# Decoder trunk on one core: cache copies taken out of the samples' steps, late window rows awaited later, and the samples' softmax divided behind the values

## The chip, the core and the metric

The kernel runs on one core of a Trainium2 chip. The metric is the device time of one execution in microseconds (us); lower is better. Matrix products run on TensorE (PE; its weight loads are PEld), elementwise work and reductions on VectorE (DVE), activations and scaled copies on ScalarE (ACT), cross-partition work on GpSimd (POOL). SyncE (SP) computes nothing here and issues nearly all DMA transfers, in the order of its program.

## The reference, cut to what matters

One layer of a decoder trunk, in float32, for 256 prompt rows and for 8 samples of 4 new rows each (width 1024). The part that the change touches is the windowed attention of the samples:

```python
def _dilated_branch_sample(q, k_all, v_all, window, dil, rel_bias):
    ...
    logits = jnp.einsum('bthd,btjhd->bhtj', q, kg, preferred_element_type=jnp.float32) + bias[None, :, None, :]
    logits = jnp.where(valid[None, None], logits, NEG)
    lse = jax.nn.logsumexp(logits, axis=-1)
    p = jnp.exp(logits - lse[..., None])
    o = jnp.einsum('bhtj,btjhd->bthd', p.astype(v_all.dtype), vg)
    return o, lse.transpose(0, 2, 1)
...
        xs = xs + _mix_out(o_a, o_b, w_out[l])
        xs = xs + _cross_attn(_rmsnorm(xs, g_x[l]), cache_mem_k[l], cache_mem_v[l], w_xq[l], w_xo[l])
        xs = xs + _moe(_rmsnorm(xs, g_ff[l]), *moe_w)
        n_new = k.shape[1]
        kw_s.append(k_all[:, n_new:])
        vw_s.append(v_all[:, n_new:])
```

There are three branches (window and dilation 128/1, 512/4, 2048/16), 8 heads of 64. The outputs `k_win_sample` and `v_win_sample` are each sample's old window of 2048 rows moved on by its 4 new rows, so nearly all of both caches is written out again. After the attentions a router sends each of the 288 rows to 4 of 32 experts, whose weights (12 MB each, float32) are read from DRAM in full.

## The kernel before, in words

Every engine has its own program, written out in order by hand, with semaphores between them; no scheduler reorders it. The stages are: norm and input projection; seven sample steps `for b in range(1, DEC_B)`; the output projection `w_out` (`out`); cross-attention (`xq` first); router; experts 0 to 31.

**A sample step b** holds, side by side, the scores of sample b and the values of sample b-1, one unit of the prompt's attention (`scores`, `logits`, `share`, `turned`, `unit_values`), and "fills" (`FILL`): pieces of the prompt's memory keys (`mk`) and values (`mv`), 16 matmuls each, which have nothing to do with the samples. For sample b, PE multiplies out the query for each of 4 tokens t (`row(b, t)` on PE, job `qb`), DVE multiplies it with the window's keys in two products and reduces the result (`row` on DVE: L1169, L1170, then the reduction L1176). `logits(b)` on DVE belongs to the prompt unit. POOL finds the maximum, ACT takes exponentials (`sample_exp`). DVE then adds them up per partition (`sums`, L1145), POOL adds over partitions, and DVE divides (`shares`, L1149 and L1150); these quotients `pr` are PE's stationary operand in `values` (L1684, 12 matmuls, and L1682, 4). DVE masks the result (`keep`, L1161) and PE turns it (`turn_values`, L1692, job `pvt`).

**Windows.** A sample's keys (K) and values (V) come as 128x2048 plus three 32x2048 transfers (L512, L515) into one buffer each. SP issues V(b) when the values matmuls of b-1 are through, and K(b+1) when the scores of b are. ACT then forms the last 128 rows of each ("late" rows, L787) by copying them; DVE waits for `late_k` ahead of the first product of a sample, PE for `late_v` ahead of the first value matmul.

**Banks.** PSUM products go round a ring of 7 banks (`TURN = 7`). The list `jobs`, filled by `add`, gives job number n the bank n % 7. `take(pe, ...)` makes PE wait until the job 7 places earlier has been read out of that bank. Bank 7 (`sx_bank`) lies outside of the ring.

**Copies.** The moved-on caches are written by 32 copies from DRAM to DRAM of 2044 KB each (`copy`, L494), issued by SP between its other transfers. `COPIES` says how many go at each of 14 places; what is left goes in `copy(len(pieces))` right behind `step0()`, which issues the first expert's weights; the loop over the other experts (L628) follows. The loads of the identity matrix and of the input rows stand at the head of SP's program.

Of the kernel before, what the change touches and what calls it, by code (L numbers as in the profile page):

```python
# [8 lines left out]
P = 128  # L9
# [43 lines left out]
def constants():  # L53
# [22 lines left out]
    col = np.arange(AW)  # L76
    own = ((p[:, None] // 32 == p[:, None] // 8 % 4) & (p[:, None] % 8 == col[None, :] // HD)).astype(np.float32)
    diag = np.concatenate([own, (p[:, None] // 32 == np.arange(DEC_T)[None, :]).astype(np.float32)], 1)
# [20 lines left out]
def build(nc, i, o):  # L99
# [5 lines left out]
    with ctx:  # L105
# [86 lines left out]
        zs = small[:, 320:352]  # L192
        zz = small[:, 352:384]
        stat = small[:, 384:440]

        own = hn[:, 2, 0:AW + DEC_T]
# [79 lines left out]
        COPIES = [5, 1, 3, 1, 2, 2, 2, 2, 2, 2, 3, 2, 1, 3]  # L276
# [30 lines left out]

        add("pt", DEC_B - 1)
        add("pvt", DEC_B - 2), add("o", DEC_B - 1), add("out", 0, 0), add("out", 0, 1), add("pv", DEC_B - 1)
# [99 lines left out]
        zpart = sem("zpart")  # L409
        zall = sem("zall")  # L410
        prob = sem("prob")
# [56 lines left out]

        block = ctx.enter_context(nc.Block())
# [3 lines left out]
        def _(sp):  # L473
            load(sp, "ident", ident[:, :], i["c_ident"])
            for t in (0, 2, 1):
# [177 lines left out]
        def _(pool):  # L653
# [23 lines left out]
            for b in range(DEC_B):  # L677
# [8 lines left out]
                pool.wait_ge(zpart, b + 1)  # L686
                nc.gpsimd.partition_all_reduce(zz, zs, P, bass.bass_isa.ReduceOp.add).then_inc(zall, 1)
# [60 lines left out]
        def _(act):  # L748
# [12 lines left out]

            act.wait_ge(consts, 2)
# [97 lines left out]

            def sample_out(b):
# [14 lines left out]
            for b in range(1, DEC_B):  # L876
                unit_pt(b - 1)
                if b >= 2:
                    sample_out(b - 2)
# [4 lines left out]
                unit_out(b - 1)  # L884
                unit_exp(b)
# [4 lines left out]
            unit_pt(DEC_B - 1)  # L890
            sample_out(DEC_B - 2)
            unit_out(DEC_B - 1)
            late_values(DEC_B - 1)
            sample_exp(DEC_B - 1)
# [3 lines left out]
            for t, (t0, n) in enumerate(TOK):  # L898
                if t == 1:
                    sample_out(DEC_B - 1)  # L900
# [109 lines left out]
        def _(dve):  # L1010
# [132 lines left out]
            def sums(b):  # L1143
                dve.wait_ge(sexp, b + 1)
# [893 lines left out]
```

## Time and profile before

| | us |
|---|---|
| time, median of 3 runs | 1411.29 |
| the 3 runs | 1403.95 to 1412.52 |
| profiled execution: its own time | 1409.75 |
| profiled execution: span | 1408.0 |
| PE busy | 1255.7 (89%) |
| DVE busy | 481.2 (34%) |
| ACT busy | 230.3 (16%) |
| chain that ended last: DMA, PE, DVE | 55%, 35%, 5% |

The profile is one execution; its span runs from the first to the last instruction and its own time is 1.75 us longer. Busy shares are over the whole span, of which the experts take the last two thirds. Positions below are in us from the start of the span: the sample steps lie at about 97 to 254, `out` and cross-attention follow, the second expert's weights are asked for at 467. "L1684" is a line of the kernel before.

### The profile page before, as it was taken

How to read it: one execution, taken by the hardware profiler on the slowest of the kernel's cores; microseconds unless marked ns; L12 is line 12 of the kernel's file. 1: busy time of each engine (PE TensorE's matmuls, PEld its weight loads, DVE VectorE, ACT ScalarE, POOL GpSimd, SP SyncE). 2: the span in 40 equal slices, each digit the busy share in tenths (PEclk: the TensorE clock that was granted, in tenths of full speed). 3: DMA queues.
4: the chain of work that ended last, by engine and by line, in shares of the span. 5: the costliest groups of instructions: out<-in, count | busy, mean ns of one | idle time of the engine just before them, and what ended most of it. 6: DMA issues, size and time to landing. Idle time of an engine off the chain costs nothing.

```text
span 1408.0 us, 16530 instructions
## 1 busy us (share of the span) xinstructions
PE 1255.7 (89%) x6407; PEld 528.5 (38%) x6407; DVE 481.2 (34%) x1037; ACT 230.3 (16%) x448; POOL 67.7 (5%) x69
## 2 busy tenths in 40 slices
PE   7989877989897999998999989999899998999986
PEld 5444323456644433333333333333333333333332
DVE  2387888332326412312232122321223212132124
ACT  1334443211311110110110100110011010011102
POOL 2010000005007000000000000000000000000000
PEclk9999988999997999999999999999999999999998
DMA  9999999998989699999999999999999999999993
GB/s 339 353 381 363 399 397 379 361 370 306 360 354 344 254 431 427 427 429 426 429 428 429 429 429 429 428 430 427 430 427 430 427 429 428 429 429 429 429 428 158
DMA packets 51740, 557.14 MB, mean 396 GB/s; under 512 B 7021, under 2 KB 9301, under 8 KB 15885
## 3 DMA queue, kind: packets, MB, share of 16 engines
q1 hardware_dynamic: 50629, 553.04, 96.0%
q0 software_dynamic: 1072, 3.57, 0.6%
q8 instruction: 26, 0.43, 0.1%
q14 instruction: 13, 0.11, 0.0%
HBM read 552.02 MB, written 71.72 MB: 443 GB/s over the span
## 4 chain that ended last, share of the span: by engine, by line
DMA 55%; PE 35%; DVE 5%; ACT 2%; issue 1%; SPq 1%; DVEq 0%; ACTq 0%; PEldq 0%
DMA wide<-in_w_gate_up 49%; PE bank L1954 12%; DMA wide<-in_cache_v_win 3%; PE bank L1642 3%; PE bank L1983 2%; PE bank L1684 2%; PE bank L1749 2%; PE bank L1512 2%; PE bank L1508 1%; PE bank L1662 1%; DMA slim<-in_w_xq 1%; DMA slim<-in_w_xv 1%; ACT wide L787 1%; PE bank L1737 1%; PE bank L1791 1%
## 5 line engine op out<-in xcount | busy, mean ns | idle before, releaser
L1954 PE MATMUL bank<-wide,att 128*64 128x512 f32 x2048 | 463.3, 596 | 58.5 <-DMA wide<-in_w_gate_up 58.3
L1954 PEld LDWEIGHTS bank<-wide,att 128*64 128x64 f32 x2048 | 139.3, 136 | 362.5 <-issue 228.8
L1983 PE MATMUL bank<-slim,att 128*64 128x512 f32 x1024 | 226.8, 595 | 0.0
L1422 DVE TENSOR_SCALAR att<-bank 128x512 f32<-128x512 f32 x32 | 22.1, 691 | 469.0 <-PE bank L1954 469.0
L1983 PEld LDWEIGHTS bank<-slim,att 128*64 128x64 f32 x1024 | 70.6, 137 | 152.2 <-issue 149.2
L1401 DVE TENSOR_TENSOR x<-x,bank 128x512 f32<-128x512 f32 x68 | 46.6, 685 | 233.1 <-PE bank L1936 226.4
L980 ACT ACTIVATE att<-att 128x512 f32<-128x512 f32 x32 | 20.2, 630 | 517.6 <-DVE att L1422 517.6
L1936 PE MATMUL bank<-tb,att 128*128 128x512 f32 (+1 forms) x192 | 84.7, 611 | 1.8 <-ACT tb L989 1.3
L989 ACT ACTIVATE tb<-bank 64x512 f32<-64x512 f32 x64 | 37.8, 591 | 234.1 <-PE bank L1983 233.7
L1662 PE MATMUL bank<-slim,ta 128*128 128x512 f32 x128 | 57.8, 601 | 0.5 <-DMA slim<-in_w_xv 0.3
L1176 DVE TENSOR_REDUCE small<-wide 128x24 f32<-128x1536 f32 x28 | 49.1, 1753 | 1.0
L1684 PE MATMUL bank<-wide,pr 128*32 128x512 f32 x192 | 33.0, 840 | 17.5 <-ACT wide L787 11.4
L1903 PE MATMUL bank<-att,mkT 128*128 128x128 bf16 x408 | 46.3, 223 | 1.4 <-DVE att L1352 1.4
L1903 PE MATMUL bank<-att,ta 128*128 128x128 bf16 x408 | 45.7, 222 | 0.0
L787 ACT ACTIVATE wide<-wide 32x512 f32<-32x512 f32 x60 | 37.6, 626 | 44.3 <-DMA wide<-in_cache_v_win 24.5
L1169 DVE TENSOR_TENSOR wide<-wide,bank 128x1024 f32<-128x1024 f32 x28 | 33.9, 1210 | 6.0 <-PE bank L1568 3.9
L1662 PEld LDWEIGHTS bank<-slim,ta 128*128 128x128 f32 x128 | 23.4, 190 | 33.4 <-issue 29.7
L1903 PEld LDWEIGHTS bank<-att,mkT 128*128 128x128 bf16 x408 | 28.3, 99 | 15.2 <-issue 14.6
L1749 PE MATMUL bank<-ta,slim 128*128 128x288 f32 x128 | 31.6, 408 | 2.7 <-DMA slim<-in_w_xq 1.8
L1429 DVE TENSOR_TENSOR att<-att 128x512 f32<-128x512 f32 x32 | 33.4, 1044 | 1.1
L985 ACT ACTIVATE att<-bank 128x512 f32<-128x512 f32 x32 | 19.1, 597 | 74.9 <-PE bank L1974 74.9
L1974 PE MATMUL bank<-ident,att 128*128 128x128 f32 x128 | 21.0, 286 | 11.5 <-DVE att L1429 9.6
(290 smaller groups left out, 1153.1 us busy)
## 6 DMA issues: line engine op xcount, KB each, us to landing
wide<-in_w_gate_up SPq DMA_DIRECT2D x128, 2048.0 KB, 25.4
slim<-in_w_down SPq DMA_DIRECT2D x64, 2048.0 KB, 22.0
out_k_win_sample<-in_cache_k_win SPq DMA_DIRECT2D x16, 2044.0 KB, 25.3
out_v_win_sample<-in_cache_v_win SPq DMA_DIRECT2D x16, 2044.0 KB, 22.9
wide<-in_w_in SPq DMA_DIRECT2D x8, 1024.0 KB, 15.8
wide<-in_cache_v_win SPq DMA_DIRECT2D x8, 1024.0 KB, 7.5
wide<-in_cache_mem_k SPq DMA_DIRECT2D x8, 1024.0 KB, 24.4
wide<-in_cache_mem_v SPq DMA_DIRECT2D x8, 1024.0 KB, 14.7
```

Source lines behind the costliest of these rows:

```text
L787: ins = A(late[32 * s:32 * s + 32, :], win[96:128, s, :], ACT.Copy)
L989: ins = A(ye[i // 2][CAP * (i % 2):CAP * (i % 2) + CAP, 512 * h:512 * h + 512], bank_y[CAP * h:CAP * h + CAP, :], ACT.Copy)
L1176: link(V.tensor_reduce(S_[b % 2][:, :, t, :], pd.rearrange("p k (h d) -> p k h d", d=HD), AX.X, ALU.add))
L1401: ins = V.tensor_tensor(dst, dst, bk[:, :], ALU.add)
L1642: ins = M(tk[h][0][0:n, :], left[:, k, t0:t0 + n], slim[:, k, 512 * h:512 * h + 512], start=k == 0, stop=k == KC - 1)
L1662: ins = M(ps[:, :], ta[:, k, P * t:P * t + P], slim[:, k, 512 * h:512 * h + 512], start=k == 0, stop=k == KC - 1)
L1684: ins = M(ps[g, :], flat[:, kind, :], vwin[:, 8 if kind == 2 else 4 * kind + t, :], start=k == 0, stop=False)
L1749: ins = M(ps[:, 0:T], slim[:, k, P * c:P * c + P], ta[:, k, :], start=k == 0, stop=k == KC - 1)
L1903: M(bk[:, c:c + 2 * CAP], hparts[t][:, s, P * k:P * k + P], onehot[:, t, :], start=t == 0 and s == 0, stop=False)
L1936: ins = M(out, back[buf][:, t0:t0 + m], ye[buf][:, 512 * h:512 * h + 512], start=True, stop=True)
L1954: ins = M(bk[half[h], :], rows[:, k, :], wide[:, k, c:c + 512], start=False, stop=k == KC - 1)
L1983: ins = M(bank_y[half[h], :], aT[:, f % 4, f // 4, :], slim[:, f, 512 * h:512 * h + 512], start=f == 0, stop=f == KC - 1)
```

## The change

- `COPIES`: one copy more before the first step (6 instead of 5 at its first place), one fewer at the third place, one fewer in each of the steps 2, 4, 5 and 6; one more at each of two places in cross-attention and the router, and three instead of one left for the place behind `step0`.
- The identity matrix and one block of input rows are loaded from ACT's queue instead of SP's; the mask `c_diag` shrinks from 128x516 to 128x32.
- DVE awaits `late_k` only ahead of the product that uses the late rows; PE takes the late rows third and awaits `late_v` there.
- `sums`, the addition on POOL, `shares` and `keep` on DVE go. PE forms the sums with 16 one-column matmuls ahead of the values (the same stationary `pr`, streaming a column of ones, into column b of bank 7), DVE takes one reciprocal of 128x1 (`part_of_sum`), and `keep` becomes a scaled copy on ACT. `turn_values` is 8 matmuls with 64 columns of weights instead of 4 with 128. Values start when the exponentials are there.
- `pvt` moves behind `unit_values`, on PE and in `jobs`, and the end of the last step is put in another order. One small product (`toep`) moves ahead of ten others. The prompt's shares stay on DVE.

The core of the diff:

```diff
-        COPIES = [5, 1, 3, 1, 2, 2, 2, 2, 2, 2, 3, 2, 1, 3]
+        COPIES = [6, 1, 2, 1, 1, 1, 1, 1, 2, 2, 4, 2, 2, 3]
...
             add("qb", b, 2), add("pt", b - 1)
+            for f in FILL[b, 0]:
+                add(*f)
+            add("qb", b, 3), add("o", b - 1)
             if b >= 2:
                 add("pvt", b - 2)
-            for f in FILL[b, 0]:
-                add(*f)
-            add("qb", b, 3), add("o", b - 1), add("s", b, 0), add("s", b, 1)
+            add("s", b, 0), add("s", b, 1)
...
+            def keep(b):
+                if b:
+                    b_, use = place(("pvt", b - 1))
+                    act.wait_ge(bank_full[b_], use + 1)
+                act.wait_ge(rz_in, b + 1)
+                ps, s = product(act, "pv", b)
+                A(kept, ps[:, :], ACT.Copy, scale=rz[:, b:b + 1]).then_inc(s, 1)
...
+            def part_of_sum(b):
+
+                b_, use = place(("pv", b))
+                dve.wait_ge(bank_full[b_], use + 1)
+                V.reciprocal(rz[:, b:b + 1], sx_bank[:, b:b + 1]).then_inc(rz_in, 1)
...
+                    if t == 0:
+                        dve.wait_ge(late_k, b + 1)
                     V.tensor_tensor(pd[:, 2, :], kw[:, 8, :], ps[:, :], ALU.mult).then_inc(s, 1)
...
             def values(b):
-                pe.wait_ge(prob, b + 1)
+                pe.wait_ge(sexp, b + 1)
+                pe.wait_ge(rz_in, b)
                 pe.wait_ge(v_in, 64 * (b + 1))
-                pe.wait_ge(late_v, b + 1)
                 ps, s = take(pe, "pv", b)
...
-                for k, kind in enumerate((2, 0, 1, 3)):
+                for kind in range(4):
+                    for t in range(DEC_T):
+                        n = NS if kind == 3 else P
+                        M(sx_bank[32 * t:32 * t + 32, b:b + 1], flat[0:n, kind, :], ones[0:n, 0:1], start=kind == 0, stop=kind == 3,
+                          tile_position=(0, 32 * t))
+                for k, kind in enumerate((0, 1, 2, 3)):
+                    if kind == 2:
+                        pe.wait_ge(late_v, b + 1)
...
             turned(DEC_B - 1)
-            turn_values(DEC_B - 2)
             unit_values(DEC_B - 1)
             round_[0] = 3
             read_out(pe, "o", DEC_B - 1)
             rows_times("out", 0, tb, P, 0)
+            turn_values(DEC_B - 2)
             values(DEC_B - 1)
```

How the order of instructions changes is shown at three places. First PE in step 3, from the fills to the values of sample 2, with the bank numbers of the ring and the waits. L1568 (L1563 after) is a query's product for one token, L1668 (L1663) a fill, L1692 (L1696) `turn_values`, L1684 (L1686) the values, L1676 the one-column matmuls; L1615 and L1591 belong to the prompt unit. Before:

```order
L1668 MATMUL bank2<-ident,hn 128x128 [waits bank_free2,bank_free6]
L1668 MATMUL bank2<-ident,hn 128x128 x3
L1568 MATMUL bank3<-hn 128x512 [waits bank_free3]
L1615 MATMUL bank4<-scr,att 64x128 [waits bank_free4,bank_free6]
L1615 MATMUL bank4<-scr,att 64x128
L1591 MATMUL bank5<-att 128x256 [waits bank_free5]
L1591 MATMUL bank6<-att 128x256 [waits bank_free6]
L1568 MATMUL bank0<-hn 128x512 [waits bank_free0]
L1568 MATMUL bank1<-hn 128x512 [waits bank_free1]
L1684 MATMUL bank2<-wide,pr 32x512 [waits late_v,bank_free2,v_in,prob]
```

After:

```order
L1563 MATMUL bank2<-hn 128x512 [waits bank_free2]
L1610 MATMUL bank3<-scr,att 64x128 [waits bank_free3,bank_free6]
L1610 MATMUL bank3<-scr,att 64x128
L1696 MATMUL bank4<-hn,wide 64x4 [waits bank_free4,bank_free3]
L1696 MATMUL bank4<-hn,wide 64x4 x7
L1586 MATMUL bank5<-att 128x256 [waits bank_free5]
L1586 MATMUL bank6<-att 128x256 [waits bank_free6]
L1563 MATMUL bank0<-hn 128x512 [waits bank_free0]
L1563 MATMUL bank1<-hn 128x512 [waits bank_free1]
L1676 MATMUL bank7<-ones,pr 32x1 [waits v_in,bank_free2,rz_in,sexp]
```

The values' bank 2 was last used by a fill before, and is last used by the query of the fourth token, `qb(3, 3)`, after the change.

Second, DVE in step 3, over the same time: L1169 and L1170 (L1164 and L1167 after) are a token's two products, L1176 (L1175) its reduction, L1121 and L1125 (L1130 and L1134) the prompt unit's `logits`. Before:

```order
L1161 TENSOR_TENSOR wide<-bank,hn 128x512 [waits dve_done,bank_full5]
L1169 TENSOR_TENSOR wide<-wide,bank 128x1024 [waits bank_full4]
L1170 TENSOR_TENSOR wide<-wide,bank 128x512
L1176 TENSOR_REDUCE small<-wide 128x3x8 [waits bank_free4]
L1145 TENSOR_REDUCE small<-pr 128x32 [waits sexp,dve_done]
L1169 TENSOR_TENSOR wide<-wide,bank 128x1024 [waits bank_full0]
L1170 TENSOR_TENSOR wide<-wide,bank 128x512
L1176 TENSOR_REDUCE small<-wide 128x3x8 [waits bank_free0]
L1149 RECIPROCAL small<-small 128x32 [waits zall,dve_done]
L1150 TENSOR_TENSOR pr<-pr,small 128x128 [waits dve_done]
L1121 TENSOR_TENSOR scr<-bank,att 128x128 [waits bank_full5,bank_full4]
```

After:

```order
L1156 RECIPROCAL small<-bank 128x1 [waits dve_done,bank_full5]
L1164 TENSOR_TENSOR wide<-wide,bank 128x1024 [waits bank_full4]
L1167 TENSOR_TENSOR wide<-wide,bank 128x512
L1175 TENSOR_REDUCE small<-wide 128x3x8 [waits bank_free4]
L1164 TENSOR_TENSOR wide<-wide,bank 128x1024 [waits bank_full0,dve_done]
L1167 TENSOR_TENSOR wide<-wide,bank 128x512
L1175 TENSOR_REDUCE small<-wide 128x3x8 [waits bank_free0]
L1130 TENSOR_TENSOR scr<-bank,att 128x128 [waits bank_full5,bank_full4,dve_done]
L1130 TENSOR_TENSOR scr<-bank,att 128x128 [waits bank_full6]
L1134 TENSOR_REDUCE small<-scr 128x1 [waits bank_free5]
L1134 TENSOR_REDUCE small<-scr 128x1 [waits bank_free6]
L1164 TENSOR_TENSOR wide<-wide,bank 128x1024 [waits bank_full2]
```

Four of DVE's instructions have gone from the step, and a short reciprocal has come; the last row after the change is the fourth token's first product, from bank 2.

Third, SP ahead of the first step: L494 (L491 after) are the copies, L512 (L509) is the window of keys of the next sample. Before:

```order
L494 DMA out_k_win_sample<-in_cache_k_win 16x8x4088 x2
L494 DMA out_v_win_sample<-in_cache_v_win 16x8x4088 x2
L494 DMA out_k_win_sample<-in_cache_k_win 16x8x4088
L373 DMA att<-toep_dram 128x8x256 [waits squares,toep_out]
L498 DMA slim<-in_w_xk 128x1024 x6
L494 DMA out_k_win_sample<-in_cache_k_win 16x8x4088
L512 DMA wide<-in_cache_k_win 128x2048 [waits w_read]
```

After:

```order
L491 DMA out_k_win_sample<-in_cache_k_win 16x8x4088 x2
L491 DMA out_v_win_sample<-in_cache_v_win 16x8x4088 x2
L491 DMA out_k_win_sample<-in_cache_k_win 16x8x4088 x2
L372 DMA att<-toep_dram 128x8x256 [waits squares,toep_out]
L495 DMA slim<-in_w_xk 128x1024 x6
L491 DMA out_v_win_sample<-in_cache_v_win 16x8x4088
L509 DMA wide<-in_cache_k_win 128x2048 [waits w_read]
```

Ahead of the window K(1) there stand seven copies instead of six.

## Rows read from the trace of the kernel before

**Rows 1.** Busy by stretch: PE, PEld, DVE, ACT, POOL; then clock, DMA share, GB/s.

```profile
97.00:250.00 153.00, 124.70 (x584) 54.69 (x584) 129.96 (x194) 64.28 (x148) 10.04 (x19) 0.89 1.00 383
205.00:210.00 5.00, 5.00 (x29) 1.12 (x22) 4.83 (x9) 2.50 (x4) 0.43 (x1) 0.68 1.02 384
250.00:455.00 205.00, 180.23 (x975) 112.73 (x971) 71.86 (x152) 41.68 (x87) 48.30 (x32) 0.91 0.93 352
455.00:467.00 12.00, 10.12 (x85) 6.62 (x84) 7.06 (x44) 0.95 (x6) 0.00 (x0) 0.76 0.04 16
560.00:1300.00 740.00, 679.46 (x3555) 243.67 (x3553) 177.10 (x390) 75.79 (x122) 0.00 (x0) 1.00 1.01 428
```

**Rows 2.** SP's issues of copies: start, duration, engine, line, tile.

```profile
32.73 1.34 SPq L494 DMA_DIRECT2D out_k_win_sample<-in_cache_k_win  x2
...
35.40 0.60 SPq L494 DMA_DIRECT2D out_k_win_sample<-in_cache_k_win  x1
```

**Rows 3.** DMA issues at 32.7:33.2 and 35.3:36.1: KB each, us to landing.

```profile
out_k_win_sample<-in_cache_k_win SPq DMA_DIRECT2D x1, 2044.0 KB, 14.9
...
out_k_win_sample<-in_cache_k_win SPq DMA_DIRECT2D x1, 2044.0 KB, 37.4
```

**Rows 4.** Chain of waits at the first sample step.

```profile
84.83 8.81 DMA wide<-in_cache_k_win
...
97.51 1.22 DVE wide L1169
```

**Rows 5.** SP's issues of V windows 1, 3 and 7.

```profile
120.42 0.33 SPq L512 DMA_DIRECT2D wide<-in_cache_v_win  x1
...
166.22 0.33 SPq L512 DMA_DIRECT2D wide<-in_cache_v_win  x1
...
251.24 0.33 SPq L512 DMA_DIRECT2D wide<-in_cache_v_win  x1
```

**Rows 6.** Chain of waits, step b=5.

```profile
190.52 10.34 DMA wide<-in_cache_v_win
```

**Rows 7.** PE in step b=5; idle before each, with releaser, in brackets.

```profile
188.72 7.13 PE L1662 MATMUL bank<-slim,ta 128*128 128x512 f32 x16
...
196.36 0.95 PE L1692 MATMUL bank<-hn,wide 128*128 128x4 f32 x8
...
199.99 0.61 PE L1568 MATMUL bank<-hn 96*128 96x512 bf16 x2 [1.44 <-DVE wide L1170]
203.68 4.99 PE L1684 MATMUL bank<-wide,pr 128*32 128x512 f32 x24 [3.09 <-ACT wide L787]
208.61 1.06 PE L1682 MATMUL bank<-att,pr 32*32 32x512 f32 x8
```

**Rows 8.** DVE in step b=5.

```profile
192.19 0.69 DVE L1161 TENSOR_TENSOR wide<-bank,hn 128x512 f32<-128x512 f32 x1 [0.21 <-DVE pp L1139]
...
197.83 0.37 DVE L1145 TENSOR_REDUCE small<-pr 128x32 f32<-128x128 f32 x1 [1.44 <-ACT pr L859]
...
199.96 1.75 DVE L1176 TENSOR_REDUCE small<-wide 128x24 f32<-128x1536 f32 x1
201.75 0.35 DVE L1149 RECIPROCAL small<-small 128x32 f32<-128x32 f32 x1
...
203.66 1.21 DVE L1169 TENSOR_TENSOR wide<-wide,bank 128x1024 f32<-128x1024 f32 x1
204.79 0.68 DVE L1170 TENSOR_TENSOR wide<-wide,bank 128x512 f32<-128x512 f32 x1
```

**Rows 9.** PE, values of sample 0.

```profile
116.59 2.78 PE L1684 MATMUL bank<-wide,pr 128*32 128x512 f32 x24
```

**Rows 10.** PE, values of sample 6 and start of cross-attention.

```profile
245.74 4.45 PE L1684 MATMUL bank<-wide,pr 128*32 128x512 f32 x24 [5.64 <-ACT wide L787]
...
305.80 4.39 PE L1749 MATMUL bank<-ta,slim 128*128 128x288 f32 x17 [1.81 <-DMA slim<-in_w_xq]
```

**Rows 11.** SP's issue of the second expert's weights.

```profile
467.00 6.96 SPq L628 DMA_DIRECT2D wide<-in_w_gate_up  x2
```

More of the change, by code:

```diff
@@ L473, in _ @@
         def _(sp):
-            load(sp, "ident", ident[:, :], i["c_ident"])
-            for t in (0, 2, 1):
+            for t in (0, 2):
                 t0, n = TOK[t]
@@ L878, in _ @@
                 if b >= 2:
-                    sample_out(b - 2)
+                    keep(b - 2)
                 sample_exp(b - 1)
@@ L890, in _ @@
             unit_pt(DEC_B - 1)
+            unit_out(DEC_B - 1)
+            keep(DEC_B - 2)
+            sample_exp(DEC_B - 1)
+            late_values(DEC_B - 1)
             sample_out(DEC_B - 2)
-            unit_out(DEC_B - 1)
-            late_values(DEC_B - 1)
-            sample_exp(DEC_B - 1)
             act.wait_ge(stored["mk"], 16)
@@ L899, in _ @@
                 if t == 1:
+                    keep(DEC_B - 1)
                     sample_out(DEC_B - 1)
@@ L1191, in _ @@
             dve.wait_ge(k_in[0], 64)
-            dve.wait_ge(late_k, 1)
             for t in range(DEC_T):
@@ L1200, in _ @@
             dve.wait_ge(k_in[1], 64)
-            dve.wait_ge(late_k, 2)
             row(1, 0), shift(0)
@@ L1214, in _ @@
                         share(0, 1, P)
-                    if t < 3:
-                        (shift, sums, shares)[t](b - 1)
-                    if b >= 2 and t == 0:
-                        keep(b - 2)
+                    if t == 0 and b > 1:
+                        shift(b - 1)
+                        part_of_sum(b - 2)
                     if t == 2:
@@ L1223, in _ @@
             share(DEC_B - 1, DEC_B, P * (UNITS[DEC_B - 1][1] + 1))
-            shift(DEC_B - 1), keep(DEC_B - 2), sums(DEC_B - 1), shares(DEC_B - 1)
+            shift(DEC_B - 1), part_of_sum(DEC_B - 2)
             for u in range(2):
@@ L1252, in _ @@
                 if t == 0:
-                    keep(DEC_B - 1)
+                    part_of_sum(DEC_B - 1)
                 norm(5 + t, n, x[0:n, t, :], hn[0:n, t, :], 6 + t)
@@ L1491, in _ @@
             pe.wait_ge(rb_rep, 1)
+            ps, s = take(pe, "toep")
+            M(ps[0:HEADS, 0:TOEP], rb, cb[:, 0:TOEP], start=True, stop=True).then_inc(s, 1)
             for kind in range(6):
@@ L1497, in _ @@
                 M(sx_bank[0:NS, 304 + 8 * t:312 + 8 * t], cb[:, c:c + NS], rb, start=True, stop=True)
-            ps, s = take(pe, "toep")
-            M(ps[0:HEADS, 0:TOEP], rb, cb[:, 0:TOEP], start=True, stop=True).then_inc(s, 1)
             for t in range(3):
@@ L1690, in turn_values @@
                 ps, s = take(pe, "pvt", b)
-                for c in range(4):
-                    ins = M(ps[:, 4 * c:4 * c + 4], kept[:, P * c:P * c + P], own[:, AW:AW + DEC_T], start=True, stop=True)
+                if b == 0:
+                    pe.wait_ge(loaded["diag"], 16)
+                for h in range(HEADS):
+                    ins = M(ps[64 * (h % 2):64 * (h % 2) + 64, 4 * (h // 2):4 * (h // 2) + 4], kept[:, HD * h:HD * h + HD],
+                            own[:, DEC_T * h:DEC_T * h + DEC_T], start=True, stop=True)
                 ins.then_inc(s, 1)
@@ L1706, in _ @@
                 turned(b - 1)
-                if b >= 2:
-                    turn_values(b - 2)
                 for f in FILL[b, 0]:
@@ L1712, in _ @@
                 unit_values(b - 1)
+                if b >= 2:
+                    turn_values(b - 2)
                 scores(b)
```

42 lines of the change are left out of this document (13 added, 29 removed).

## The prediction

> **What bounds the kernel now.** I read the busy times by stretch first, to see which resource has no slack where, then the chain of waits for what a step ends on, then PE, DVE and SP in one sample step. Over the experts the DMA share is 1.01 at 428 GB/s, and PE is busy 679 of 740 us. That stretch has no slack in the queue, and the change doesn't touch it: the end moves by as much as the second expert's weights start earlier or later, at 467.00 [rows 11]. Just before that, from 455 to 467, the DMA share is 0.04: the queue is empty, and it is PE and DVE that are late. So time saved in the steps reaches the end one for one, as long as the queue isn't made late itself. During the steps (97 to 250) the queue has a share of 1.00, DVE is busy 130 of 153 us and PE 125 [rows 1]: three resources near their limits, and which of them closes a step is the question.
>
> Before, it is the V window. V lands 10.34 us after its last issue, behind two copies [rows 6], ACT copies its late rows, PE has waited 3.09 us for them, and the values (4.99 + 1.06 us) end where the next V is issued [rows 7]. Six such intervals last from 120.42 to 251.24: 45.8 us for the first two, 85.0 for the last four, which hold the mv fills [rows 5].
>
> **Copies.** A copy costs the queue 6.3 us: the first of five lands at 32.73 + 14.9 = 47.6, the last, issued just behind 35.40, at 35.4 + 37.4 = 72.8, and 25.2 / 4 = 6.3 [rows 2, 3]. One fewer in steps 4 to 6 brings V forward by about that, more than the 3.09 us that PE waits: the V wait goes, and it is no longer what is late.
>
> The copy that is added at the first place stands ahead of K(1). K(1) is on the chain: it lands at 84.83 + 8.81 = 93.64, the late rows follow on ACT, and DVE's first product starts at 97.51 [rows 4]. So this copy delays the first step by up to 6.3 us. To its credit stand a smaller mask (my estimate from the copy's price and size: 0.4 us) and two loads fewer at the head of SP's program (0 to 1 us). I take **+5.0**, bounds +4.3 to +6.3. That DVE awaits `late_k` only at the third product doesn't help: a product of ACT that PE waits for stands behind the late rows in ACT's order, so the first product is as late as ever.
>
> The Trainium skill, "DMA: Bandwidth & Descriptors", section "Issuing engines are not separate DMA queues", says that a load started from another engine runs on the same DMA engines and saves only the time of issuing it. By that rule the two loads on ACT are worth nothing in the queue, and the credit would be 0.4; the trace of before has no such load to test it.
>
> Four copies net go from the steps to behind 250. The queue has 7% of 205 us idle there, 14 us, and 11.5 of the 12 us ahead of 467 [rows 1]: 26 us for 4 x 6.3 = 25. It fits just, though not exactly where the idle lies. The two copies behind `step0` fill the gap ahead of 467; of the two earlier ones some part is absorbed, and the queue comes free at about 473 instead of 467. SP's first two issues there take 6.96 us before [rows 11], since the second one awaits a buffer, so most of these 6 us lie beside that wait. I take **+0.7**, bounds 0 to +6.
>
> **DVE.** A step loses keep 0.69, sums 0.37 with a wait of 1.44 for ACT's exponentials, a reciprocal 0.35, and a multiplication about as long [rows 8]. A reciprocal of 128x1 comes; about 3.0 us go in all. Of the 20.8 us from V to V, DVE's own list then fills 17.7. POOL's addition and its wait vanish with it; ACT takes on the scaled copy, some 0.7 us, with 3 us to spare before V's landing.
>
> **PE's new wait.** The bank numbers show one that the diff doesn't name. `pv(b-1)` now takes the bank of `qb(b,3)`, so the values of b-1 can't begin before DVE has finished the third product of the fourth token (the row that begins at 203.66 before [rows 8]); before, the bank had last held a fill that had long been read. Behind the values stand, on PE, the fill and then the next step's third-token query, which DVE needs. This makes a closed loop between PE and DVE: values 2.78 + 1.06 at full clock [rows 9] or 4.99 + 1.06 at low clock [rows 7]; the one-column matmuls, u; a fill, 7.13 less its overlap with what follows, or 7.0 [rows 7]; a query 0.4; then on DVE the third token, 1.21 + 0.68 + 1.75, or 3.6, logits about 1.05 (1.3 between the divisions and 203.66, less for the prompt units with one tile), and the fourth token's products, 1.8 [rows 8]. Without u: 17.6 at full clock, 19.8 at low.
>
> u has no row. 16 matmuls make 32 records. Four column groups can run side by side, as the values' do (24 records of 512 columns in 2.78 us). Then there are 8 rounds: `turn_values` has 8 records with four columns in 0.95 us [rows 7], with four times the weight columns, so 0.45 to 0.95. One after the other at that row's pace it would be 3.8 us. I take **0.7**, since the column groups are what the values use too, with the same stationary tile. So a step is 18.3 at full clock and 20.5 at low.
>
> "TensorEngine Tiling (Array Packing)" in the Trainium skill, section "Instruction Overhead", states that a matmul with one streamed column takes as long as one with 60. By that, 8 rounds stay within the 0.7, and 32 in a line give the rival below; no row here has a one-column product.
>
> **The sum**, at low clock in the values, as before shows it (granted clock 0.68 in 205 to 210 [rows 1]). First two intervals: about +0.1 (the one-column matmuls against DVE's relief). Of the last four (85.0): the first, which held other waits as well, -1.5; the next two from 20.8 to 20.5, -0.6 together; the last -4.5, since the values of sample 6 take another bank and wait no longer for V, where 5.64 us stand before [rows 10]. With +5.0 of the first copy that is -1.5 when V(7) is issued. After that, `turn_values` (0.95) and the one-column matmuls (0.7) stand among the `out` products, +1.65, and the 1.81 us wait for w_xq [rows 10] goes, as w_xq no longer trails so many copies; with +0.7 from the late copies, about -1.
>
> The clock decides over the rest. At full clock in the values five steps gain 2.2 us each, 11 more, to about -12 at most. Before, PE idles 1.44 and 3.09 us ahead of the values [rows 7] and the clock is low; after, it waits about 4 us in the same place, for DVE. So low remains likelier; I count some 30% of the steps at full, -3. **Forecast: -4 on the profiled 1409.75, or 1406.** Its own range is 1401 to 1411. The profiled execution stands 1.5 below the median of 1411.29; a run of before at 1403.95 shows how far one execution strays, and differences under about 1% (14 us) can hardly be told from no change.
>
> **Rivals.**
>
> *The clock stays up, or the bank wait costs nothing.* If the values run at full clock all through, steps are 18.3; if besides the one-column products hide, they follow DVE's list at 17.7. Five steps of 2.2 to 2.8 us on top of -1: 1395 to 1399. For it: PE has less to wait for in all. Against it: the wait is gathered in one place.
>
> *The one-column matmuls run one after the other (slower).* 32 records in a line at that row's 119 ns make u 3.8, and at half of it, for a stationary tile a quarter as wide (an estimate), 1.9. From u = 1.0 at low clock a step exceeds 20.8, and every step loses. At 1.9 it is +1.2 at each of seven places, +8 on the sum; at 3.8 +3.1, or +22. That gives 1417 to 1430, slower than before. For it: all use the same 128 rows of the array. Against it: the values' four groups do run side by side.
>
> *The copies are given back late.* If the queue comes free at 473 and nothing hides it, +6 instead of +0.7: 1411. For it: 26 us of idle for 25 of copies is no margin. Against it: the second expert's weights aren't needed at once, since PE has the whole of expert 0 before it.
>
> **Chances.** Forecast 0.48, clock or DVE's list 0.22, copies given back 0.15, one after the other 0.15. Faster by over 1% (below 1397) takes the better half of the first rival and a little of the forecast for an unknown I haven't priced: 0.18. Slower by over 1% (above 1425) needs the upper third of this slow rival: 0.05. The range, 1396 to 1418, leaves out the lower end of the one and the upper half of the other.
>
> **What would show it.** V waits ahead of the values gone, in their place an idle time of PE ended by DVE's L1167; V(1) about 5 us later than 120.42, and V(7) near 250; steps of 20.5 us where the clock is low in the values and 18.3 where it isn't; the one-column matmuls side by side in under 1 us; the queue busy up to 470 and more, with no gap from 455. Wrong would be: steps that end in a V wait still (a copy priced too low), a K(1) that DVE doesn't wait for, and a stream of weights that starts much later than 473.

## The result and the profile after

The changed kernel takes 1414.46 us in the median of 17 runs (1412.69 to 1417.75), the kernel before 1406.59 in 17 (1402.61 to 1412.52): a ratio of 1.0054, interval 1.0041 to 1.0067. The time lies in the range that was given, but the forecast was 0.3% faster than the kernel before, and it came out 0.54% slower. The profiled execution of the changed kernel takes 1412.69 with a span of 1410.9, 2.9 us more than before. Single executions of these two kernels lie up to 5.9 us off their own medians (of the kernel before, two profiled ones took 1409.75 and 1409.74, some 3 us above its median), so the traces are good for tracing where the mechanism went, and the ratios for how much.

Busy times by stretch in the changed kernel, to set beside [rows 1]; the last three columns are granted clock, DMA share and GB/s:

```profile
97.00:110.00 13.00, 6.79 (x26) 4.85 (x26) 5.92 (x11) 7.92 (x16) 2.86 (x4) 0.50 1.02 426
97.00:250.00 153.00, 129.38 (x864) 59.73 (x864) 117.58 (x167) 71.36 (x159) 6.03 (x11) 0.86 0.79 314
250.00:455.00 205.00, 179.07 (x1010) 110.32 (x1006) 73.67 (x155) 42.97 (x89) 47.78 (x31) 0.91 1.01 375
455.00:467.00 12.00, 10.02 (x82) 7.75 (x84) 5.61 (x36) 0.95 (x6) 0.34 (x1) 0.66 1.01 372
```

The queue that was full from 97 to 250 now idles a fifth of that time, and what idled later is full: 1.01 from 250 to 467, with no gap left ahead of the second expert. The first row is the surprise: TensorE ran at 0.50 for the whole first stretch of the steps, its lower level of 1.2 GHz.

The chain of waits at the first step shows why, beside [rows 4]. The window of keys lands at 80.75 + 18.09 = 98.84, 5.2 us later than before:

```profile
80.75 18.09 DMA wide<-in_cache_k_win
```

PE at the same place; the number in brackets is how long it had idled, and what ended it:

```profile
80.47 10.46 PE L1569 MATMUL bank<-wide,ta 128*128 128x512 f32 x24
102.16 1.19 PE L1563 MATMUL bank<-hn 96*128 96x512 bf16 x2 [11.23 <-ACT att L769]
```

PE is through with its front at 90.9 and stands still for 11.23 us, for a product of ACT that comes behind the late rows of the window. Behind that the clock is low: 0.51 over 94 to 110 and 0.76 from there to 120, where the kernel before has 1.00 in both in the execution shown. A second execution of it has 0.68 over 94 to 110 (last run below).

SP's issues of the windows V(1), V(3), V(6) and V(7), as in [rows 5]:

```profile
129.28 0.33 SPq L509 DMA_DIRECT2D wide<-in_cache_v_win  x1
...
174.91 0.33 SPq L509 DMA_DIRECT2D wide<-in_cache_v_win  x1
...
236.14 0.33 SPq L509 DMA_DIRECT2D wide<-in_cache_v_win  x1
...
250.36 0.33 SPq L509 DMA_DIRECT2D wide<-in_cache_v_win  x1
```

V(1) is 8.9 us later than before, the next two intervals take 45.6 (45.8 before), the last four 75.5 (85.0), and V(7) is 0.9 earlier. One step in the middle, PE, beside [rows 7]:

```profile
205.49 0.60 PE L1563 MATMUL bank<-hn 96*128 96x512 bf16 x2
209.82 0.71 PE L1676 MATMUL bank<-ones,pr 128*32 128x1 f32 x32 [3.72 <-DVE wide L1167]
210.45 4.46 PE L1686 MATMUL bank<-wide,pr 128*32 128x512 f32 x24
```

and DVE over the same time, beside [rows 8]:

```profile
202.90 1.22 DVE L1164 TENSOR_TENSOR wide<-wide,bank 128x1024 f32<-128x1024 f32 x1 [2.52 <-PE bank L1563]
...
207.86 1.21 DVE L1164 TENSOR_TENSOR wide<-wide,bank 128x1024 f32<-128x1024 f32 x1
208.99 0.68 DVE L1167 TENSOR_TENSOR wide<-wide,bank 128x512 f32<-128x512 f32 x1
```

No wait for V is left. PE waits 3.72 us for DVE's L1167 ahead of the one-column products, that is for the third product of the fourth token, whose bank it wants. DVE in turn waited 2.52 us for the query at 202.90 that stands behind the fill on PE. The 32 records of the one-column products take 0.71 us.

The end of the steps. DVE's last score rows and the prompt's last share:

```profile
243.47 1.22 DVE L1164 TENSOR_TENSOR wide<-wide,bank 128x1024 f32<-128x1024 f32 x1 [3.04 <-PE bank L1563]
...
252.94 0.74 DVE L1140 TENSOR_TENSOR scr<-scr,small 128x512 f32<-128x512 f32 x1
```

and PE around it, with the output projection (L1637; before it starts at 254.10) and the first product of cross-attention (L1754, beside [rows 10]):

```profile
249.24 1.06 PE L1684 MATMUL bank<-att,pr 32*32 32x512 f32 x8
253.73 1.16 PE L1600 MATMUL bank<-hn,scr 128*128 128x128 f32 x8 [3.44 <-DVE scr L1140]
...
257.09 16.26 PE L1637 MATMUL bank<-slim,tb 128*128 128x512 f32 x32 [0.39 <-ACT tb L837]
...
308.80 1.78 PE L1754 MATMUL bank<-ta,slim 128*128 128x288 f32 x3 [0.69 <-DVE ta L1055]
```

The values of sample 6 are through at 250.3, and PE then stands 3.44 us for the prompt's last share. `out` starts 3.0 us later than before, runs with the clock low in its first part (granted 0.53 over 257 to 262; 16.26 us for 32 products, 14.00 before at 1.00), and cross-attention starts 3.0 us later than in [rows 10]. The second expert's weights are asked for at 468.85 (467.00 in [rows 11]), and they land 10.6 us after their issue, where it was 7.2 before. The columns are size and us from issue to landing:

```profile
wide<-in_w_gate_up SPq DMA_DIRECT2D x1, 2048.0 KB, 10.6
```

### The profile page after: what moved, and what is told of

The parts are those of the page before. It is cut to its first block, busy times and chain, and to the rows that moved or that the text cites. A ratio compares the mean times of both kernels' runs of the same rounds, so it can differ in the third digit from the quotient of the medians.

```text
span 1410.9 us, 17140 instructions
## 1 busy us (share of the span) xinstructions
PE 1257.9 (89%) x6727; PEld 530.2 (38%) x6727; DVE 470.8 (33%) x1013; ACT 235.4 (17%) x456; POOL 63.5 (5%) x61
## 4 chain that ended last, share of the span: by engine, by line
DMA 51%; PE 35%; DVE 7%; SPq 5%; issue 1%; ACT 1%; DVEq 0%
DMA wide<-in_w_gate_up 49%; PE bank L1959 12%; PE bank L1657 4%; PE bank L1637 3%; PE bank L1988 2%; SPq L495 2%; PE bank L1754 2%; PE bank L1686 2%; SPq L372 1%; DMA wide<-in_cache_k_win 1%; DVE wide L1164 1%; DMA hn<-in_mem_prompt 1%; PE bank L1742 1%; PE bank L1941 1%; DVE small L1175 1%
## 5 line engine op out<-in xcount | busy, mean ns | idle before, releaser
L989 ACT ACTIVATE att<-att 128x512 f32<-128x512 f32 x32 | 20.2, 630 | 518.5 <-DVE att L1417 518.5
L1175 DVE TENSOR_REDUCE small<-wide 128x24 f32<-128x1536 f32 x28 | 49.1, 1753 | 1.0
L1164 DVE TENSOR_TENSOR wide<-wide,bank 128x1024 f32<-128x1024 f32 x28 | 33.9, 1211 | 31.7 <-PE bank L1563 31.6
L1754 PE MATMUL bank<-ta,slim 128*128 128x288 f32 x128 | 33.3, 425 | 0.7 <-DVE ta L1055 0.7
L1686 PE MATMUL bank<-wide,pr 128*32 128x512 f32 x192 | 30.7, 789 | 0.0
## 6 DMA issues: line engine op xcount, KB each, us to landing
out_v_win_sample<-in_cache_v_win SPq DMA_DIRECT2D x16, 2044.0 KB, 27.6
```

Source lines behind the costliest of these rows:

```text
L1164: V.tensor_tensor(pd[:, 0:2, :], pair, ps[:, :].unsqueeze(1).broadcast_to([P, 2, AW]), ALU.mult)
L1175: link(V.tensor_reduce(S_[b % 2][:, :, t, :], pd.rearrange("p k (h d) -> p k h d", d=HD), AX.X, ALU.add))
L1686: ins = M(ps[g, :], flat[:, kind, :], vwin[:, 8 if kind == 2 else 4 * kind + t, :], start=k == 0, stop=False)
L1754: ins = M(ps[:, 0:T], slim[:, k, P * c:P * c + P], ta[:, k, :], start=k == 0, stop=k == KC - 1)
```

## The experiments

Twelve runs followed. Ratios are to the kernel before on the same chip, with a 95% interval; the changed kernel stands at 1.0054. The expectations name times beside 1406.6 for the kernel before; in the second set of four runs its median was 1408.6, in the third 1407.1, so go by the ratios.

### The copies, apart and together

Four kernels differ from the changed one or from the one before in the list alone:

```diff
 changed        [6, 1, 2, 1, 1, 1, 1, 1, 2, 2, 4, 2, 2, 3]
 before         [5, 1, 3, 1, 2, 2, 2, 2, 2, 2, 3, 2, 1, 3]
+first_back     [5, 1, 3, 1, 1, 1, 1, 1, 2, 2, 4, 2, 2, 3]  in the changed kernel
+late_back      [6, 1, 2, 1, 2, 2, 2, 2, 2, 2, 3, 2, 1, 3]  in the changed kernel
+copies_back    [5, 1, 3, 1, 2, 2, 2, 2, 2, 2, 3, 2, 1, 3]  in the changed kernel
+copies_only    [6, 1, 2, 1, 1, 1, 1, 1, 2, 2, 4, 2, 2, 3]  in the kernel before
```

`first_back`, what was expected:

> The changed kernel with one number moved back: the copy that was added ahead of K(1) goes where it was, behind the first windows (places one and three of COPIES are 5 and 3 again); the four copies that were moved behind the steps stay there. Reference points: before 1406.6, changed 1414.5. Three theories. START (the loss is the first step, which begins 5 us later and at the lower clock, V(1) issued at 129.3 instead of 120.4): 1406, V(1) near 120. LATE QUEUE (the loss is the copies given back behind 250, where the queue of the changed kernel has no gap left, share 1.01 in every stretch): 1412 to 1415, the earlier first step is lost again at the queue. REWRITING (the loss lies in the bank wait and the one-column products, the copies are even): 1414.

1.0023 (1.0007 to 1.0038), 1409.7 us. By the medians more than half of the loss is this one copy: 0.31 of 0.54%. START had expected all of it. V(1) and V(7):

```profile
122.62 0.33 SPq L509 DMA_DIRECT2D wide<-in_cache_v_win  x1
...
243.99 0.33 SPq L509 DMA_DIRECT2D wide<-in_cache_v_win  x1
```

Both are 6.4 to 6.7 us earlier than in the changed kernel. V(1) is still 2.2 us later than in the execution shown of the kernel before (0.4 earlier than in its second one), though the window of keys now lands earlier, at 91.9 instead of 93.6: PE idles 4.0 us ahead of it instead of 11.2, and the clock is 0.57 over 94 to 110. The same waits of PE, summed over the span (total, times, longest):

```profile
PE bank L1676 <- DVE wide L1167: 12.2, 5, 3.7
...
PE bank L1563 <- ACT att L769: 4.0, 1, 4.0
```

`late_back`, what was expected:

> The changed kernel with the other half of the copies put back: steps 2, 4, 5 and 6 get their second copy again, and the places behind the steps lose one each (one copy is left behind the first expert's weights); the extra copy ahead of K(1) stays. START: 1414, since the first step is as late as in the changed kernel. LATE QUEUE: 1406 to 1408, with an empty queue ahead of 467 again and steps that are no longer than 20.8. REWRITING: 1414.

1.0049 (1.0028 to 1.0069), 1413.0 us: beside the changed kernel a gain that can't be told from none. LATE QUEUE as the main cause falls.

`copies_back`, what was expected:

> The changed kernel with the list of copies of the kernel before; everything else is as changed. START: 1406. LATE QUEUE: 1406 or somewhat less. If both hold and add up: 1400. REWRITING: 1414. Steps wait for V again (V lands some 10 us after its issue), at 20.5 to 21 us each.

1.0010 (0.9993 to 1.0026), 1408.7 us. With the old list, all the rest of the change together can't be told from no change. V is hardly waited for, 0.7 us in one step, where the expectation had steps that wait for V again. The bank wait is there as in the changed kernel:

```profile
PE bank L1676 <- DVE wide L1167: 12.4, 5, 3.7
```

`copies_only`, what was expected:

> The kernel before with the list of copies of the changed kernel; nothing else is changed. START and LATE QUEUE: 1412 to 1416, as slow as the changed kernel or slower, V(1) near 126. REWRITING: 1406, or less, since the V wait goes and DVE's list of 19 us a step takes its place.

1.0039 (1.0021 to 1.0056), 1411.7 us. REWRITING as the only cause falls too: the list alone makes the old code slower, by an amount that can't be told from the changed kernel's. The V wait has gone, but the steps are 20.0 to 20.8 us as ever, from V(3) to V(7), since PE now waits for DVE's sums and shares. PE in one step:

```profile
204.09 0.60 PE L1568 MATMUL bank<-hn 96*128 96x512 bf16 x2 [1.45 <-DVE wide L1170]
206.59 5.27 PE L1684 MATMUL bank<-wide,pr 128*32 128x512 f32 x24 [1.89 <-DVE pr L1150]
```

V(1) is later than expected, at 130.14 and not near 126. The two loads are still SP's here and PE's front is as late as before, yet PE idles 8.16 us for the late window, and the clock is 0.66 over 94 to 110 and 0.70 to 120. PE's first query product behind the window, and V(1):

```profile
103.65 1.19 PE L1568 MATMUL bank<-hn 96*128 96x512 bf16 x2 [8.16 <-ACT att L772]
```

```profile
130.14 0.33 SPq L512 DMA_DIRECT2D wide<-in_cache_v_win  x1
```

### The bank, the other side of the loop, the front

`ring`: the values take an older bank.

```diff
             add("s", b, 0), add("s", b, 1)
             if b + 1 < DEC_B:
-                add("qb", b + 1, 0), add("qb", b + 1, 1)
+                add("qb", b + 1, 0)
             add("pv", b - 1)
+            if b + 1 < DEC_B:
+                add("qb", b + 1, 1)
...
-                    row(b + 1, 0), row(b + 1, 1)
+                    row(b + 1, 0)
                 values(b - 1)
+                if b + 1 < DEC_B:
+                    row(b + 1, 1)
```

> The changed kernel with the bank wait taken out: the values of sample b-1 come ahead of the second token's query of sample b+1, in the program of PE and in the list of jobs, so that they take a bank that was read out long before, and the query takes the bank of the fourth token. Reference: changed 1414.5. LOOP (the closed loop of PE and DVE sets the steps, and what they lose the end loses): PE no longer waits 1.3 to 3.7 us for DVE's L1167 ahead of the one-column products, steps go from 20.3 to 18 or 19, 1405 to 1408. START (the loss is made ahead of the first step and what the steps gain is lost again at their end): V(1) as late as in the changed kernel at 129, out(0) at most 2 us earlier than 257, 1412 to 1415.

0.9963 (0.9944 to 0.9981), 1403.1 us: 0.9% below the changed kernel and faster than the kernel before. V(3), V(4), V(5) and V(7):

```profile
169.71 0.33 SPq L511 DMA_DIRECT2D wide<-in_cache_v_win  x1
...
186.46 0.33 SPq L511 DMA_DIRECT2D wide<-in_cache_v_win  x1
...
203.62 0.33 SPq L511 DMA_DIRECT2D wide<-in_cache_v_win  x1
...
237.40 0.33 SPq L511 DMA_DIRECT2D wide<-in_cache_v_win  x1
```

Steps of 16.8, 17.1, 19.4 and 14.4 us (V(6) at 222.97), and V(7) 13 us earlier than in the changed kernel. The one-column products follow the query at once, and no wait for L1169, the third product here, stands ahead of them in any step:

```profile
197.43 0.39 PE L1565 MATMUL bank<-hn 96*128 96x512 bf16 x1 [0.77 <-DVE wide L1169]
197.75 0.61 PE L1678 MATMUL bank<-ones,pr 128*32 128x1 f32 x32
```

LOOP holds, with more gain than it had expected (1405 to 1408), and START with its first step as the only loss falls: V(1) is as late as in the changed kernel (129.84), and `out` starts at 245.21, 11.9 us earlier than there. The edit also moves the values ahead of one query on PE, since a job's place in the list gives its bank.

`row2`: the third token's query goes ahead of the fill, on PE and in the list of jobs, and the bank stays shared. The part on PE (the same move in `jobs` is left out):

```diff
             for b in range(1, DEC_B):
-                row(b, 2)
+                if b == 1:
+                    row(b, 2)
                 turned(b - 1)
...
                 values(b - 1)
+                if b + 1 < DEC_B:
+                    row(b + 1, 2)
                 for f in FILL[b, 1]:
                     fill(f)
```

> The changed kernel with the loop cut at its other side: PE multiplies the third token's query of the next sample ahead of the 7 us fill instead of behind it, so that DVE doesn't wait for the fill; the values still take the bank of the fourth token. Reference: changed 1414.5. LOOP: DVE's own list of 17.7 us sets the steps, and its tail before out(0) comes earlier with it: 1400 to 1406. START: 1412 to 1415.

1.0058 (1.0037 to 1.0078), 1417.9 us: no gain. DVE doesn't wait for that query any longer, but the loop closes through the prompt's scores, which stand behind the fill as well. DVE's `logits` with its wait:

```profile
209.10 0.76 DVE L1134 TENSOR_TENSOR scr<-bank,att 128x256 f32<-128x256 f32 x2 [2.28 <-PE bank L1590]
```

and PE's scores (L1590) and the next one-column products:

```profile
208.27 0.70 PE L1590 MATMUL bank<-att 64*128 64x256 f32 x4
...
212.38 0.71 PE L1680 MATMUL bank<-ones,pr 128*32 128x1 f32 x32 [2.87 <-DVE wide L1171]
```

So LOOP's figures failed here, and the trace shows why: this cut was in the wrong place of a loop that stays closed, from the end of the scores over `logits`, the fourth token's products, the values and the fill back to the scores.

`early_window`: the list [4, 1, 4, 1, 2, 2, 2, 2, 2, 2, 3, 2, 1, 3] in the changed kernel.

> The changed kernel with the copies of the kernel before, but 4 instead of 5 of them ahead of the first window of keys (and 4 instead of 3 behind it). In the changed kernel PE is through with its front at 91 and idles 11 us for that window, at the lower clock afterwards. Reference: 1408.7 with 5, 1414.5 as changed. START: the window lands 6 us earlier than with 5, the first rows start at 92 instead of 96, the clock stays up in the first step: 1401 to 1404. Rival (the queue has to carry the copy in any case, right behind the window): 1408.

1.0026 (1.0007 to 1.0046), 1413.0 us, so START's expectation failed and the rival's was not far off. The first step does begin earlier (the first query at 91.4, no longer waiting for the window), with a clock of 0.79 over 94 to 110, but the four copies right behind it stand ahead of V(1), which lands 21.54 us after its last issue; V(2) is issued later than before. SP's issues of V(1) and V(2), and the chain between them:

```profile
117.83 0.33 SPq L509 DMA_DIRECT2D wide<-in_cache_v_win  x1
...
150.76 0.33 SPq L509 DMA_DIRECT2D wide<-in_cache_v_win  x1
```

```profile
119.50 21.54 DMA wide<-in_cache_v_win
```

`loads_back`: the two loads return to SP.

```diff
-            for t in (0, 2):
+            load(sp, "ident", ident[:, :], ident_rows)
+            for t in (0, 2, 1):
...
-            load(act, "ident", ident[:, :], ident_rows)
-            load(act, "x1", x[:, 1, :], second_rows)
```

> The changed kernel with the identity matrix and the second block of input rows loaded by SP again. The changed kernel's PE runs some 5.5 us ahead of the kernel before from the first input product (12.4 instead of 17.7) up to 91, where it waits for the window of keys. START: PE comes 2 to 5 us later to the same wait, which costs nothing, and the lower clock behind it is shorter: 1411 to 1415. Rival (the front counts): slower by those 2 to 5 us, 1417 to 1420.

1.0074 (1.0049 to 1.0098), 1419.8 us; the intervals overlap with the changed kernel's. PE's first input product starts at 17.17 as in the kernel before (17.72), in the changed kernel at 12.38:

```profile
17.17 4.21 PE L1502 MATMUL bank<-ta,wide 128*128 128x288 f32 x8
```

```profile
12.38 3.87 PE L1503 MATMUL bank<-ta,wide 128*128 128x288 f32 x8
```

So the front is faster by nearly 5 us through two loads. How much of that shows in the time these intervals don't tell. START had a shorter stretch of lower clock when PE comes later to the same wait, and that bought nothing. PE idles 6.72 us instead of 11.23, the window lands at 100.16 instead of 98.84, the clock is 0.79 over 94 to 110 and 0.66 to 120, and V(1) comes no earlier, at 131.11 instead of 129.28. PE's first query product behind the window, and V(1):

```profile
103.49 1.19 PE L1562 MATMUL bank<-hn 96*128 96x512 bf16 x2 [6.72 <-ACT att L768]
```

```profile
131.11 0.33 SPq L510 DMA_DIRECT2D wide<-in_cache_v_win  x1
```

### The three together

`ring_first`: `ring` and `first_back` together.

> The changed kernel with two edits: the bank wait taken out (as in the run that had this alone, 0.9963 of the kernel before), and the added copy moved back behind the first windows (alone: 1.0023, where the changed kernel stands at 1.0054). If the first step and the bank wait are two separate losses, they add up: 0.993, some 1397 to 1399 beside 1407 for the kernel before. LATE QUEUE (the queue, full from V(7) on, eats what comes earlier): 0.996, as with the bank wait alone.

0.9944 (0.9930 to 0.9958), 1399.1 us: 0.6% below the kernel before and 1.1% below the changed one. Its two edits gained 0.31% and 0.91% apart; together it is 1.10%. V(1) and V(7):

```profile
122.87 0.33 SPq L511 DMA_DIRECT2D wide<-in_cache_v_win  x1
...
233.07 0.33 SPq L511 DMA_DIRECT2D wide<-in_cache_v_win  x1
```

and the landing of the second expert's first weights, 14 us behind their issue at 449.16 (10.6 in the changed kernel), with the queue full there (DMA share 1.00 from 455 to 467):

```profile
wide<-in_w_gate_up SPq DMA_DIRECT2D x1, 2048.0 KB, 14.0
```

`ring_copies_back`: `ring` with the list of the kernel before.

> The changed kernel with the bank wait taken out and the list of copies of the kernel before, two in each step. THREE LIMITS (the V window behind two copies, DVE's list with the softmax in it and the bank wait each close a step at about 20.5; only with all three gone does it fall to 17): steps of 19.5 to 20.5, waits for V ahead of the values, 1406 to 1409. LOOP alone: 1397 to 1400, since the copies don't matter to the steps.

0.9974 (0.9960 to 0.9989), 1404.4 us. As THREE LIMITS had it, V is waited for again, 2.74, 4.69 and 5.15 us in three steps. The steps are 17.9 to 22.7 us, though, where it had 19.5 to 20.5, and the time lies between its forecast and LOOP's:

```profile
198.10 0.71 PE L1678 MATMUL bank<-ones,pr 128*32 128x1 f32 x32 [2.74 <-DMA wide<-in_cache_v_win]
...
219.54 0.71 PE L1678 MATMUL bank<-ones,pr 128*32 128x1 f32 x32 [4.69 <-DMA wide<-in_cache_v_win]
...
241.89 0.71 PE L1678 MATMUL bank<-ones,pr 128*32 128x1 f32 x32 [5.15 <-DMA wide<-in_cache_v_win]
```

Fewer copies in the steps are worth their place in the kernel whose other two limits are gone: there going from the old list to that of `ring_first` gives 0.3%. With the bank wait still in, the same two lists are `copies_back` (1.0010) and `first_back` (1.0023), and no gain shows. In the old code this list was not run; the changed one, with the copy ahead of K(1), cost 0.4% there.

`ring_fill` has the list [5, 1, 3, 1, 2, 1, 1, 2, 2, 2, 4, 2, 1, 3] in `ring`.

> The bank wait taken out, the added copy moved back, and two of the late copies given to two steps in which the queue still idles half of the time (places five and eight of the list). LATE QUEUE: the queue behind the steps has 12 us less to carry: 1393 to 1396, below the same kernel without this. Rival (V waits behind the second copy in these two steps): as that kernel, 1397 to 1400.

0.9949 (0.9935 to 0.9963), 1400.9 us, as `ring_first`. The rival's figure holds: PE waits 3.7 us for V in one step, and V(7) is issued at 239.53 where `ring_first` has 233.07, so the steps lose 6.5 us.

`before_again`: the kernel before once more.

> The kernel before, unchanged, for a second profile: the one shown is of an execution of 1409.75, while the median of 17 is 1406.6. If what differs between executions is TensorE's clock in the steps, another execution shows other stretches of the lower clock and V(7) some us away from 251; if it is the queue, landings of copies differ with the steps equal.

1409.74 us, a span of 1408.0, V(7) at 251.1. It is the first step that differs. The window of keys lands at 93.7 in both executions and PE's first query product behind it starts at 97.0, but PE had idled 1.57 us ahead of it instead of 0.43, and the clock over 94 to 110 is 0.68 instead of 1.00. The execution shown, PE and the stretch (columns as in [rows 1]):

```profile
96.98 0.39 PE L1568 MATMUL bank<-hn 96*128 96x512 bf16 x1 [0.43 <-ACT att L772]
```

```profile
94.00:110.00 16.00, 12.12 (x58) 7.49 (x58) 9.25 (x16) 13.81 (x37) 3.04 (x5) 1.00 1.00 387
```

The second execution, PE, the stretch and V(1):

```profile
97.00 0.39 PE L1568 MATMUL bank<-hn 96*128 96x512 bf16 x1 [1.57 <-ACT att L772]
```

```profile
94.00:110.00 16.00, 12.33 (x47) 8.80 (x46) 8.86 (x14) 12.95 (x33) 2.85 (x4) 0.68 1.02 409
```

```profile
123.04 0.33 SPq L512 DMA_DIRECT2D wide<-in_cache_v_win  x1
```

So V(1) is 2.6 us later than 120.42 in the same kernel, after the same start. V(2) is issued at 144.9 instead of 148.2, but V(4) to V(7) agree within 0.6 us and so does the end, so neither of the two expectations holds. What makes other executions of it 3 us faster this doesn't show.

## Why the prediction was wrong

**What bounds the kernel**: right. The end follows the second expert's weights, and in the steps three resources lie near their limits.

**The new wait of PE**: right, in place and size. The values' bank held them up for DVE's fourth token, 12.4 us in five steps, and the steps from V(3) to V(6) came out at 20.2 to 20.7 (20.5 forecast; the loop's terms add up to 17.7 and 19.9 without u, 0.1 more than was written, which changes nothing). The one-column products, the term without a row, took 0.54 to 0.71 (0.7 taken). The rival in which they run one after the other is out: 32 records take less than the 8 of [rows 7].

**The first step**, +5.0 for the copy ahead of K(1): the landing was right, the step behind it was mis-sized. The window landed 5.2 us later (98.84 against 93.64); with the same list and front it landed at 99.2 in `late_back` and 100.7 in `row2`. The list alone made it 6.7 (100.33 in `copies_only`), so a credit of some 1 us for mask and loads is as large as that scatter. But V(1) came 8.9 later, because the time from PE's first query behind the window to V(1) grew from 23.4 to 27.1 us. The sum had no term for the clock there, which was 0.51 behind an idle time of 11.23 us. What the lower clock goes with shows in one kernel: in the second execution of the kernel before that stretch takes 26.0 us at 0.68, so 2.6 of the 8.9 are there without any change, and against that execution V(1) is 6.2 later. The earlier front is not to blame: in `loads_back` and `copies_only`, where it is as late as before, the stretch takes 27.6 and 26.5 us. In the medians the copy is worth 0.31% (`first_back`), or 4.4 us.

**The last interval**, -4.5: a wait that the sum had overlooked. The interval was 14.2 us, 6.6 below the 20.8 before, but V(7) isn't what `out` waits for. `out` waits for the prompt's last unit, and that for DVE's list of step 7 (L1140 ends at 253.7, the values of sample 6 at 250.3), which had got no shorter than the loop allows. From V(6) to the start of `out` the changed kernel takes 20.95 us (236.14 to 257.09) and the kernel before 23.70 (230.40 to 254.10): 2.75 us reached `out`, where the sum carried all of its 4.5 on. `out` started 3.0 us later than before where the sum had it 1.5 earlier. The last four intervals together gained 9.6, even more than the 6.6 that was forecast; that was counted at the wrong event.

**The clock in the values**, -3: not seen. The values of five of the eight samples took 4.3 to 4.8 us, near the low figure of 4.99 and not the 2.78 at full clock, as my own argument against it had it.

**Late copies**, +0.7: 1.0 between the first expert (471.37 against 469.50) and the end (+2.9). `late_back` (1.0049 against 1.0054) can't tell them from nothing.

**The sum** was -4; the same terms, measured, are +8.9 at V(1), -9.7 from there to V(7), +3.9 from V(7) to `out`, 0.0 to cross-attention, -1.1 to the first expert and +1.0 to the end: +2.9 in the profiled executions. So the step that failed is the way from the copy to `out` in this sum, in three terms. Up to V(6) it had +3.0, and +5.7 was measured, the first step above all. From V(6) to `out` it had -4.5, and -2.75 was measured. And -3 for the clock stood for nothing that the trace shows. These miss by 2.7, 1.8 and 3 us, and none alone turns the sign; behind `out` the sum was 0.6 too high. The medians are 7.9 us apart and not 2.9, since the profiled execution of the kernel before lies 3.2 above its median and that of the changed kernel 1.8 below; where these 5.0 us arise no trace shows. `copies_back` and `first_back` place 0.3 to 0.4% of the 0.54% in the copies.

**Why a large change moved so little.** Three limits each close a step at about 20.5 us: the V window behind two copies, DVE's list with the softmax in it, and, once the jobs stand in this order, the bank. The distance from V(4) to V(6), two steps, in each kernel, with the limits that it has:

| kernel | limits left | V(4) to V(6), us | ratio |
|---|---|---|---|
| before | V window, DVE's list | 41.6 | 1 |
| copies_only | DVE's list | 40.4 | 1.0039 |
| copies_back | V window (0.7 us of waits), bank | 40.5 | 1.0010 |
| changed | bank | 40.6 | 1.0054 |
| ring_copies_back | V window | 42.8 | 0.9974 |
| ring | none | 36.5 | 0.9963 |
| ring_first | none | 33.7 | 0.9944 |

With any one of them left these two steps take 40 to 43 us, and the time moves by 0.5% at most either way, 0.3% of it for the copy ahead of the first step. `ring_copies_back` gains a little all the same, in its first steps (V(3) at 165.8, in `first_back` at 168.6). What I had given the rival that follows DVE's list was there: without the bank wait the steps from V(3) to V(6) take 17.8 us on average (17.7 forecast for it) and V(7) comes 13 us earlier. How much of that the end keeps is open: by the medians 0.91%, or 12.8 us, nearly all of it; between the two profiled executions 7.2 us, with the second expert's weights asked for 9.6 us earlier. I had seen the bank and counted it as a loop of the same length as before, but not as the one thing between this change and a gain.

## What to carry to other kernels

Where several resources close a loop at nearly the same period, price a change by the one that is left, and look through the tables that hand out buffers for a wait that no line of the diff shows: it decided here over the gain of everything else. Credit time saved at an event only if the next stage waits for that event; here V(7) came earlier and `out` waited for something else. Price a window that comes later with the step behind it, not with its landing alone: PE idled for it, and with the lower clock behind that the step took 2.6 to 4.2 us more than the 23.4 at full clock. And take a second trace of the kernel before: V(1) differed by 2.6 us between two executions of it, as much as several terms of the sum.

## What the runs showed that I had not expected

Two loads, of the identity matrix and of one block of input rows, moved from SP to ACT, brought the first input product forward by 4.8 us (12.38 against 17.17 in `loads_back`), though a load takes SP some 0.4 us to issue. The block of input rows was issued 0.9 us earlier (1.18 against 2.11) and landed 2.8 earlier (6.9 against 9.7). The products ahead of the first input product, from the small transposes on, took 3.3 us (9.12 to 12.38) instead of 5.5 (11.63 to 17.17) at a granted clock of 1.00 in both; why is not shown. The Trainium skill, "DMA: Bandwidth & Descriptors", section "Issuing engines are not separate DMA queues", has it that only the issuing time is saved; at this place, at the head of the program, the landing shows more than that.
